# Decay sums and beta spread over the partitions through DRAM, Gram products turned, conv-state transposes merged

## What is computed

```python
q, k = l2_norm(q), l2_norm(k)                    # behind a causal conv of width 4 and SiLU
beta = sigmoid(b);  g = -exp(a_log) * softplus(a + dt_bias)
G = cumsum(g)                                    # within a chunk
decay = exp(where(causal, G[:, None] - G[None, :], -inf))
a_mat = where(strict, (beta * k) @ k.T * decay, 0)
u = solve(I + a_mat, v * beta)                   # lower triangular
w = solve(I + a_mat, k * beta * exp(G))
qk = (q @ k.T) * decay                           # q scaled by 128 ** -0.5
# then: v_new = u - w @ S;  o = (q * exp(G)) @ S + qk @ v_new;  S = S * exp(G_last) + kd.T @ v_new
```

## Time and profile before

| what | value |
|---|---|
| median of 3 runs | 1909.12 us (1908.06 to 1911.35) |
| the profiled execution | 1911.12 us, its span 1909.3 us |
| busy: PE, DVE, ACT | 1800.0, 556.5, 388.0 us |
| busy: weight loads, POOL | 933.9, 19.5 us |
| moved | 519.92 MB, mean 272 GB/s |
| chain that ended last | PE 79%, DMA 17%, DVE 2%, ACT 1% |

### The profile page before, as it was taken

One profiled execution on the slowest core, in us unless ns is written; L12 is line 12 of the kernel. 1 busy time (PEld: TensorE's weight loads), 2 busy tenths in 40 slices (PEclk: granted clock), 3 DMA queues, 4 the chain that ended last, 5 costly groups with the idle time before them and its releaser, 6 DMA issues.

```text
span 1909.3 us, 22816 instructions
## 1 busy us (share of the span) xinstructions
PE 1800.0 (94%) x8060; PEld 933.9 (49%) x8060; DVE 556.5 (29%) x1811; ACT 388.0 (20%) x922; POOL 19.5 (1%) x37
## 2 busy tenths in 40 slices
PE   7999999999998999999999999999999999999998
PEld 4777777777775433433333333333333333334333
DVE  2334434434434200321323213232132311224113
ACT  1424524524523111311000111001010010002103
POOL 0000000000000000000000000000000000000000
PEclk9999999999999999999999999999999999999999
DMA  8333433433404461599999999999999999999401
GB/s 253 100 95 102 126 94 103 124 94 104 124 28 149 152 250 73 199 419 428 427 428 427 427 427 427 427 427 427 428 426 427 425 427 425 424 424 384 168 22 50
DMA packets 208462, 519.92 MB, mean 272 GB/s; under 512 B 18664, under 2 KB 139488, under 8 KB 157152
## 3 DMA queue, kind: packets, MB, share of 16 engines
q1 hardware_dynamic: 198160, 513.83, 69.0%
q0 software_dynamic: 2304, 4.86, 0.7%
q10 hardware_dynamic: 7968, 0.83, 0.3%
HBM read 519.14 MB, written 12.26 MB: 278 GB/s over the span
## 4 chain that ended last, share of the span: by engine, by line
PE 79%; DMA 17%; DVE 2%; ACT 1%; issue 1%; SPq 0%; DVEq 0%; ACTq 0%
PE ps L582 75%; DMA ring<-in_w_down_dram 17%; PE ps L585 3%; DMA x<-in_x_sample_dram 0%; PE ps L1082 0%; ACT hb L1210 0%; ACT ring L1210 0%; SPq L477 0%; DMA pp_rows<-hb 0%; DVE ring L1694 0%; PE ps L710 0%; PE ps L730 0%; DVE ring L1745 0%; PE ps L731 0%; DVE x L2011 0%
## 5 line engine op out<-in xcount | busy, mean ns | idle before, releaser
L582 PE MATMUL ps<-ring,hT 128*64 128x512 f32 x2048 | 457.0, 596 | 25.6 <-DMA ring<-in_w_up_dram 25.6
L582 PE MATMUL ps<-hT,ring 128*128 128x288 f32 x1536 | 410.1, 414 | 0.0
L582 PE MATMUL ps<-ring,mixT 128*64 128x512 f32 (+2 forms) x1408 | 365.6, 598 | 35.9 <-DMA ring<-in_w_down_dram 25.6
L582 PEld LDWEIGHTS ps<-hT,ring 128*128 128x128 f32 x1536 | 283.3, 192 | 70.4 <-issue 0.5
L582 PEld LDWEIGHTS ps<-ring,hT 128*64 128x64 f32 x2048 | 145.7, 137 | 308.4 <-issue 305.8
L582 PEld LDWEIGHTS ps<-ring,mixT 128*64 128x64 f32 (+2 forms) x1408 | 124.8, 144 | 240.2 <-issue 238.3
L582 PE MATMUL ps<-ring,hb 128*128 128x512 f32 (+2 forms) x512 | 143.7, 512 | 0.0
L582 PE MATMUL ps<-mixT,wpT 128*128 128x512 f32 (+1 forms) x384 | 130.1, 601 | 0.0
L582 PEld LDWEIGHTS ps<-ring 128*128 128x128 f32 (+3 forms) x880 | 115.7, 186 | 29.0 <-DVE ring L1767 7.9
L582 PE MATMUL ps<-ring 128*128 128x128 f32 (+3 forms) x880 | 123.8, 272 | 1.7 <-DVE ring L1754 1.6
L1210 ACT ACTIVATE ring<-ps 128x256 f32<-128x256 f32 (+5 forms) x176 | 47.5, 310 | 294.4 <-PE ps L582 256.8
(11 more groups left out here) (248 smaller groups left out, 1096.7 us busy)
## 6 DMA issues: line engine op xcount, KB each, us to landing
ring<-in_w_gate_dram SPq DMA_DIRECT2D x128, 1024.0 KB, 22.5
ring<-in_w_up_dram SPq DMA_DIRECT2D x128, 1024.0 KB, 24.4
ring<-in_w_down_dram SPq DMA_DIRECT2D x128, 1024.0 KB, 22.0
ring<-in_w_in_dram SPq DMA_DIRECT2D x48, 1024.0 KB, 5.6
ring<-in_w_out_dram SPq DMA_DIRECT2D x16, 1024.0 KB, 11.0
ring<-in_w_ple_gate_dram SPq DMA_DIRECT2D x16, 1024.0 KB, 13.3
hb<-in_state_delta_dram SPq DMA_DIRECT2D x8, 512.0 KB, 5.2
out_dram<-hb SPq DMA_DIRECT2D x8, 512.0 KB, 3.7
```

The costliest lines, as they stand in the source:

```text
L582: return pe.matmul(out, lhsT, rhs, start=start, stop=stop)
```

## The change

The sums G and beta of all heads are turned in the preparation by six more matmuls (8 rows of 288 columns each), copied by DVE to gb_stage, stored by SP to a DRAM buffer gb_rows, and a head's two rows are loaded from there into all 128 partitions (Gb, 2304 bytes each): for the first head right behind the store, for the others in the head before, behind load_gate. With G along the row in SBUF, DVE makes dd and its mirror dT at the head's start, and ACT takes both exponentials.

The Gram products are now computed in turned form, one matmul per tile with k as weights and q and k side by side as 256 columns. DVE multiplies them with decay, beta along the row and masks, which gives the turned matrices (NTa, QKT) directly; X, which needs the other orientation only beside the diagonal, is built from the same product, since k k^T is symmetric, with the mask low0 folded into DL. The matmuls of gcol, the six transposes of Am and QKm, the wait for A_r, AT_mm, and ACT's copy of QKT go. PE's `next_head()` calls keep their counts, so 12 and 9 projection matmuls now stand together. The level masks of NT are made one level at a time (levels 0 to 2 before the loop of levels, then lev + 2 behind each lev_new), both tiles in one operation.

The conv-state rows of q, k and v lie one below the other on 72 partitions and are turned by one transpose; so do the new rows, 81 columns, turned by one; stores read them at partitions 27 s. The diff, cut to its core:

```diff
+        gb_rows = nc.dram_tensor("gb_rows", (HEADS, 2 * TOK), F32).ap()
+            def load_rows(h):
+                sp.dma_start(Gb.rearrange("p a n -> p (a n)"), gb_rows[bass.ds(h, 1), :].to_broadcast([P, 2 * TOK])
+                             ).then_inc(E["gb_ld"], 16)
...
                 sp.wait_ge(piece_mm, s + 1)
                 load_piece(s, P + piece_col[s])
+            sp.wait_ge(dec["prep_v"], 4)
+            sp.dma_start(gb_rows, gb_stage.rearrange("p a n -> p (a n)")).then_inc(E["gb_st"], 16)
+            sp.wait_ge(E["gb_st"], 16)
+            load_rows(0)
...
                     sp.wait_ge(E["mixA_r"], h1)
                     load_gate(h1)
+                    load_rows(h1)
                 piece(3)
...
-            mm(ps[0:SAMPLE, 3, 40:48], C("ball", SAMPLE), g[0:SAMPLE, 2, :]).then_inc(dec["prep_mm"], 1)
+            mm(ps[0:SAMPLE, 3, 40:48], C("ball", SAMPLE), g[0:SAMPLE, 2, :])
+            beta = pre[:, 3]
+            for t in range(2):
+                mm(ps[0:HEADS, 3, 64 + t * P:64 + (t + 1) * P], g[:, t, :], C("triu"))
+                mm(ps[0:HEADS, 2, t * P:(t + 1) * P], beta[:, t, :], C("ident"))
+            mm(ps[0:HEADS, 3, 64 + PROMPT:64 + TOK], g[0:SAMPLE, 2, :], C("btriu", SAMPLE))
+            mm(ps[0:HEADS, 2, PROMPT:TOK], beta[0:SAMPLE, 2, :], C("ident", SAMPLE, SAMPLE)).then_inc(dec["prep_mm"], 1)
...
-                for s in range(3):
-                    last = tr(ps[:, 2, s * 24:(s + 1) * 24], stt[0:SEQS * PAD, s, :], SEQS * PAD)
-                last.then_inc(E["st_T"], 1)
+                tr(ps[:, 2, 0:72], stt[0:72, :], 72).then_inc(E["st_T"], 1)
                 pe.wait_ge(E["cs_r"], h1)
-                for s in range(3):
-                    last = tr(ps[0:27, 4, s * P:(s + 1) * P], cs[:, s, :], P)
-                last.then_inc(E["cs_T"], 1)
+                tr(ps[0:81, 4, 0:P], cs[:, :, :].rearrange("p s c -> p (s c)"), P).then_inc(E["cs_T"], 1)
...
                 for t in range(2):
-                    kt, qt = qk[:, 1, t * P:(t + 1) * P], qk[:, 0, t * P:(t + 1) * P]
-                    mm(ps[:, 7, t * P:(t + 1) * P], kt, kt)
-                    mm(ps[:, 7, 256 + t * P:256 + (t + 1) * P], qt, kt)
-                    mm(ps[:, 2, t * P:(t + 1) * P], gcol[:, t, :], C("triu"))
-                kt, qt = qk[:, 1, PROMPT:TOK], qk[:, 0, PROMPT:TOK]
-                mm(ps[0:SAMPLE, 4, 0:SAMPLE], kt, kt)
-                mm(ps[0:SAMPLE, 4, SAMPLE:2 * SAMPLE], qt, kt)
-                mm(ps[:, 2, PROMPT:TOK], gcol[0:SAMPLE, 2, :], C("btriu", SAMPLE)).then_inc(E["tok_mm"], 1)
+                    mm(ps[:, 7, t * 256:(t + 1) * 256], qk[:, 1, t * P:(t + 1) * P], qk[:, :, t * P:(t + 1) * P])
+                mm(ps[0:SAMPLE, 4, 0:2 * SAMPLE], qk[:, 1, PROMPT:TOK], qk[:, :, PROMPT:TOK]).then_inc(E["tok_mm"], 1)
                 next_head()
-
-                pe.wait_ge(E["A_r"], h1)
-                pe.wait_ge(E["tok_cp"], h1)
-                pe.wait_ge(E["D_r"], h1)
-                for t in range(2):
-                    tr(ps[:, 5, t * P:(t + 1) * P], Am[:, t, :], P)
-                    tr(ps[:, 6, t * P:(t + 1) * P], QKm[:, t, :], P)
...
                 next_head()
...
                     if lev == 1:
                         pe.wait_ge(E["NT_r"], h1)
+                        pe.wait_ge(E["tok_cp"], h1)
...
-                f(eG, ps[:, 2, 0:TOK], ACT.Exp)
-                f(Dm[:, :, :], dd[:, :, :], ACT.Exp, scale=-1.0)
-                f(Ds[0:SAMPLE, :], dds[0:SAMPLE, :], ACT.Exp, scale=-1.0).then_inc(E["D_r"], 1)
+                f(eG, Gb[:, 0, :], ACT.Exp)
+                f(dd[:, :, :], dd[:, :, :], ACT.Exp, scale=-1.0)
+                f(dds[0:SAMPLE, :], dds[0:SAMPLE, :], ACT.Exp, scale=-1.0)
+                f(dT[:, :, :], dT[:, :, :], ACT.Exp)
+                f(dTs[0:SAMPLE, :], dTs[0:SAMPLE, :], ACT.Exp).then_inc(E["D_r"], 1)
+                act.wait_ge(E["tok_mm"], h1)
...
+            cp(gb_stage[:, 0, :], ps[0:HEADS, 3, 64:64 + TOK])
+            cp(gb_stage[:, 1, :], ps[0:HEADS, 2, 0:TOK])
...
-                for t, (_, n) in enumerate(TILES):
-                    ts(gcol[0:n, t, :], C("ones", n), hs[0:n, t, 0:1], None, ALU.mult)
+                v.wait_ge(E["gb_ld"], snap(h * 16 + 16))
+                for out, sample, clip in ((dd, dds, ALU.max), (dT, dTs, ALU.min)):
+                    for t in range(2):
+                        ts(out[:, t, :], Gb[:, 0, t * P:(t + 1) * P], hs[:, t, 1:2], 0.0, ALU.subtract, clip)
+                    last = ts(sample[0:SAMPLE, :], Gb[0:SAMPLE, 0, PROMPT:TOK], hs[0:SAMPLE, 2, 1:2], 0.0, ALU.subtract, clip)
+                last.then_inc(E["dd_r"], 1)
...
+                tt(CT[:, :, :], dT[:, :, :], both("triu"), ALU.mult)
+                tt(EB[:, :, :], dT[:, :, :], Gb[:, 1, 0:PROMPT].rearrange("p (t n) -> p t n", t=2), ALU.mult)
...
+                v.wait_ge(E["tok_mm"], h1)
+                gram = ps[:, 7, :].rearrange("p (t a n) -> p t a n", t=2, a=2)
+                tt(NTa[:, :, :], gram[:, :, 1, :], EB[:, :, :], ALU.mult)
...
+                    st(out=X[:, t, :], in0=gram[:, t, 1, :], scalar=hs[:, t, 2:3], in1=DL[:, t, :], op0=ALU.mult, op1=ALU.mult)
...
+                def masked(lev):
+                    return tt(NT[:, lev, :, :], NTa[:, :, :], both(f"mt{lev}"), ALU.mult)
...
+                tt(QKT[:, :, :], gram[:, :, 0, :], CT[:, :, :], ALU.mult)
+                tt(QKTs[0:SAMPLE, :], ps[0:SAMPLE, 4, 0:SAMPLE], CTs[0:SAMPLE, :], ALU.mult).then_inc(E["QKT_r"], 1)
+                masked(2)
...
+                    if lev + 2 < LEVELS:
+                        masked(lev + 2)
```

More of the change, by code:

```diff
@@ L191, in trunk @@
         qk = w(2, TOK)
-        gcol = w(3, P)
+        Gb = w(2, TOK)
         dd = w(2, P)
         dds = w(SAMPLE)
[L195 to L198, removed]
+        dT = w(2, P)
+        dTs = w(SAMPLE)
+        DL = w(2, P)
+        DLs = w(SAMPLE)
         eG = w(TOK)
         qg = w(TOK)
[L201 to L204, removed]
+        EB = w(2, P)
+        EBs = w(SAMPLE)
+        NTa = w(2, P)
+        NTas = w(SAMPLE)
         kbg = w(3, P)
@@ L230, in trunk @@
         cs = w(3, PAD + SEQS * PAD)
-        csT = w(3, P)
-        stt = w(3, P)
+        csT = w(P)
+        stt = w(P)
         vaT = w(TOK)
@@ L247, in trunk @@
         mA = ot
[L248 to L249 removed]
+        CT = w(2, P)
+        CTs = w(SAMPLE)
+        gb_rows = nc.dram_tensor("gb_rows", (HEADS, 2 * TOK), F32).ap()
+        gb_stage = Snew[0:HEADS, 0:5, :].rearrange("p a n -> p (a n)")[:, 0:2 * TOK].rearrange("p (a n) -> p a n", a=2)
         lnj = Vm[:, 0:3, :]
@@ L315, in trunk @@
                  "cs_cp", "cs_st", "va_st", "s2_st", "sn_st", "qkv_r", "sq_r", "ss_mm", "qk_r", "tok_mm", "dd_r", "D_r",
-                 "tok_cp", "A_r", "AT_mm", "QKT_r", "NT_r", "W_r", "dS_mm", "W_T", "WT_r", "Wrep", "WTs_r", "ln_d",
+                 "tok_cp", "gb_st", "gb_ld", "QKT_r", "NT_r", "W_r", "dS_mm", "W_T", "WT_r", "Wrep", "WTs_r", "ln_d",
                  "ln_sq", "vn_r", "mixA_mm", "mixA_r", "uw_mm", "uw_cp", "WQ_r", "S1_mm", "S1_r", "SQ_mm", "wS_mm",
@@ L1668, in _, with both @@
             n_before = ch.n
+            def both(name):
+                return C(name).unsqueeze(1).to_broadcast([P, 2, P])
             def head(h, loop):
@@ L1713, in head @@
                 tt(qk[:, 1, :], qkvT[:, 1, :], rn[:, 1, :], ALU.mult).then_inc(E["qk_r"], 1)
-                v.wait_ge(E["tok_mm"], h1)
-                for t in range(2):
-                    ts(dd[:, t, :], ps[:, 2, t * P:(t + 1) * P], hs[:, t, 1:2], 0.0, ALU.subtract, ALU.max)
-                ts(dds[0:SAMPLE, :], ps[0:SAMPLE, 2, PROMPT:TOK], hs[0:SAMPLE, 2, 1:2], 0.0, ALU.subtract,
-                   ALU.max).then_inc(E["dd_r"], 1)
                 v.wait_ge(E["qk_r"], h1)
@@ L1722, in head @@
                 tt(qg, qk[:, 0, :], eG, ALU.mult)
+                st(out=DL[:, :, :], in0=dd[:, :, :], scalar=-1.0, in1=both("low0"), op0=ALU.mult, op1=ALU.mult)
+                st(out=DLs[0:SAMPLE, :], in0=dds[0:SAMPLE, :], scalar=-1.0, in1=C("low0", SAMPLE, SAMPLE), op0=ALU.mult,
+                   op1=ALU.mult)
+                tt(CT[:, :, :], dT[:, :, :], both("triu"), ALU.mult)
+                tt(CTs[0:SAMPLE, :], dTs[0:SAMPLE, :], C("btriu", SAMPLE), ALU.mult)
+                tt(EB[:, :, :], dT[:, :, :], Gb[:, 1, 0:PROMPT].rearrange("p (t n) -> p t n", t=2), ALU.mult)
@@ L1723, in head @@
+                ch(tt(EBs[0:SAMPLE, :], dTs[0:SAMPLE, :], Gb[0:SAMPLE, 1, PROMPT:TOK], ALU.mult))
+                ch.wait()
+                v.wait_ge(E["tok_mm"], h1)
+                gram = ps[:, 7, :].rearrange("p (t a n) -> p t a n", t=2, a=2)
+                tt(NTa[:, :, :], gram[:, :, 1, :], EB[:, :, :], ALU.mult)
+                tt(NTas[0:SAMPLE, :], ps[0:SAMPLE, 4, SAMPLE:2 * SAMPLE], EBs[0:SAMPLE, :], ALU.mult)
                 for t in range(2):
-                    tt(DS[:, t, :], Dm[:, t, :], C("strict"), ALU.mult)
@@ L1728, in head @@
                 ch.wait()
```

(28 more changed lines are left out.)

18 lines of the change are left out of this document (6 added, 12 removed).

## The result

The changed kernel took 1903.99 us (median of 9 runs, 1902.08 to 1906.67) against 1909.12: ratio 0.9973, 95% interval 0.9963 to 0.9982, 5.1 us less. Forecast were 10.6 us less, with 1903.5 as the upper end. So the direction was right, the size about half. The first median lies 0.5 us beyond the range's upper end and the two others, 1901.41 and 1903.14, lie inside it, so the scatter of the medians alone could have put it on either side; what is missing from the forecast gain is told from the traces.

What follows compares the result with a forecast made beforehand. PE was taken to bound the heads, with expert loads released by its progress. Seven looped heads gain 10.5 us, the last 4.9, the first loses 4.8: 10.6 less, median 1898.5 us, range 1893.5 to 1903.5.

Steps and rivals of the forecast that it cites:

- Looped heads, tokens: Token part of each looped head: shorter Gram stretch gains 0.83 us, six transposes gone gain 0.69.
- Looped heads, start: Start of each looped head: two transposes fewer, -0.23 us; DVE's later cs_r, +0.25; net +0.02; sq_r wait stays shut.
- Row load in the loop: Loading the next head's rows inside the looped heads: one more SP issue and some 295 KB, cost 0.
- First head: Start of the first head: uncovered DRAM round trip of the rows delays PE, loss 4.8 us, bounds 3.0 and 8.
- Last head: Last head, qk_r to first level: waits A_r and NT_r, transposes and Gram time go; net gain 4.9 us.
- Rival (a): Clock falls at two or three head starts, 1.7 us each; last head 1.7 either way; 1902.5 us; chance 0.12.
- Rival (b): Clock falls at every head start, 2.1 us in each of seven heads; 1913.2 us; chance 0.05.
- (c): DVE bounds the heads: PSUM-priced operations or sq_r and NT_r waits open; 5 us less gain, 1903.5; chance 0.08.
- (d): First head's round trip long, 8 instead of 4.8 us, and late in the loop too; 1901.7 us; chance 0.07.
- (e): Gain doesn't reach the end, expert loads start by something else than PE; 0 to -2 us, 1908; chance 0.06.

Runs made afterwards that it cites:

- e7: Changed kernel with its Gram products as one matmul for each product (four of 128, two of 32 columns); 1902.69 us.
- e6: Changed kernel with the merging of the conv-state transposes undone: three each for old and new conv rows; 1903.02 us.
- e2: Changed kernel with two matmuls of 288 columns, result unread, put on PE ahead of the wait for cs_r; 1899.07 us.
- after: The changed kernel itself, against the kernel before the change; 1903.99 us.
- before: The kernel without the change, the reference of the comparison; 1909.12 us.
- e9: e8 with the projection matmul behind the output steps moved to ahead of the wait for va's piece at the head's start; 1876.95 us.
- e8: e3 with projection matmuls moved from behind tok_mm: one ahead of cs_r, one ahead of or_r, three ahead of sq_r in the last head; 1886.07 us.
- e5: Kernel before the change with three more unread DVE operations of 128 columns ahead of cs_r at each head start; 1911.89 us.
- e1: Changed kernel run once more, nothing altered; 1901.41 us.
- e10: Changed kernel run a third time, nothing altered; 1903.14 us.
- e3: Changed kernel with DVE's row-load wait and six dd and dT operations moved from the head's start to behind ln_d; 1892.59 us.
- e4: Kernel before the change with three unread matmuls of 288 columns added in each head behind the steps following tok_mm; 1918.78 us.

## Why the prediction was half right

The steps hold as follows.

- *Looped heads, tokens*: 0.83 + 0.69 forecast. The Gram stretch went from 2.01 to 1.19 us, the way from there to the first level from 11.09 to 10.29, and neither NT_r nor QKT_r was waited for. Right, and 0.1 us better than forecast. The cover was less than the 6.8 us of the forecast (10.2 less 3.4): DVE reached NT_r at 168.1, PE at 172.35, 4.2 us ahead. D_r did not come before tok_mm, as the prediction had it; ACT was held by table loads and a piece, and DVE's masks began at 163.29, 1.2 us behind the Gram stretch. That it is gcol's matmuls that pay, as the sum by columns had it, e7 shows.
- *Looped heads, start*: net +0.02 forecast. PE resumed 0.18 us after cs_r's transpose instead of 0.35, with a gap of 1.20 us instead of 0.71. DVE's six operations took 1.08 us (145.58 to 146.66), forecast 1.02. sq_r stayed shut. cs_r came 0.27 us later behind the head's first transpose, forecast 0.25; but of the 0.23 us of two transposes only 0.06 stayed, as e6 shows. The net was +0.21, and that a head still shrank by 1.46 us, where 1.50 were forecast, is in part luck: the tokens gave 0.1 more than forecast and the rest of the head 0.05.
- *Row load in the loop*: cost nothing. In the first head's turn it was issued at 126.37, 19 us ahead of its use at 145.58, and such a load landed in 4.1 us (median of eight).
- *First head*: forecast -4.8, measured -5.85 to cs_r. prep_v 4 came 3.99 us behind the preparation's mark, forecast 3.98. The store took 2.2 us from issue to the load's issue (68.08 to 70.27), forecast 1.4; the load 3.4, forecast 3.2. The term of the round trip was too small by 1 us. The further loss of the first head to the low clock, taken over as it was, came out 0.3 us smaller. The Trainium skill ("DMA: Bandwidth & Descriptors", Latency and other measured facts) with its fixed cost of about 2 us for a DMA was nearer for the store than the 1.4 us row of a 16 KB store inside a stream.
- *Last head*: forecast -4.9, measured -6.5, and -5.2 in e2 where the clock fell at the old place. The waits for A_r and NT_r went as said. The 1.6 us on top are no saving of the change: in after the clock fell behind sq_r, so the slow stretch lay under the wait for qk_r, which shrank from 2.05 us to 0.49. Rival (a) had this chance, 1.7 us either way. The clock there in the table by stretch, then PE's timeline of after:

```profile
581.00:582.00 1.00, 1.00 (x3) 0.69 (x3) 0.00 (x0) 0.98 (x5) 0.00 (x0) 0.50 1.04 406
```

```profile
580.59 2.22 PE L593 MATMUL ps<-ring,cst 128*128 128x288 f32 x4 [3.07 <-ACT ring L1209]
582.60 2.37 PE L593 MATMUL ps<-hT,ring 128*128 128x288 f32 x6
585.46 0.33 PE L743 MATMUL ps<-cst,ring 128*128 128x128 f32 x1 [0.49 <-DVE ring L1721]
...
592.80 0.78 PE L593 MATMUL ps<-ring 128*128 128x128 f32 x6
```

- *The step that failed* is the price of PE's longer wait for cs_r in "Looped heads, start": it was put down at its 0.25 us alone, with the clock at 1.00, and the fall of the clock was put among the rivals, as (a), with 0.12. The fall was what happened, in three heads, at the price given there: 3 x 1.68 = 5.0 us, which e2 gave back. With it the sum is 10.6 - 5.0 - 1.0 (first head) + 1.6 (last head) = 6.2 us, inside the three intervals. The evidence given against it, clock 1.00 in all looped heads of before, was evidence on gaps of 0.7 us only.
- A side error, in the section on the kernel before as well: the 0.6 us at L710 were put down to or_r. They are ACT's emptying of the last piece behind the last projection matmul, as e9 shows for the changed kernel. It changed nothing in the sum, but misplaced a matmul in e8.

Rival (b) would have needed a fall in all seven heads. (c) is out by the head length of 70.23 us. Of (d) only 1 us in the first head came true, and nothing in the loop. (e) is out by the table: behind the heads the trace of after loses nothing of its lead.

## What to carry to other kernels

A gap of PE that grows costs more than its length where it brings the clock down: here the falls stood behind gaps of 0.91 to 1.20 us and cost 1.7 us each. Such a gap needs that price as a rival with a real chance, or work put into it. Work that fills an engine's early part of a stage (dd and dT ahead of cs_r) belongs where that engine waits anyway; the same six operations 8 us later, where DVE waited for the norms, held up nothing, and the DRAM round trip was covered with them. Where PE has surplus cover at one wait and none at another, moving single matmuls between them gains their whole length, provided they stand behind the work that the wait's releaser itself needs.

## What the runs showed of the hardware

- PE's granted clock fell to 0.50 for 3.4 us behind gaps of only 0.91 to 1.20 us (with a wait of 0.58 us shortly ahead), in one to three of seven nearly equal places (e5, e6, after, e7), and in the same places in three traces of one program (after, e1, e10). Behind gaps of 0.71 us (before, e3, e4) it fell at none.
- Two dependent DMAs of 18 KB out and 288 KB in took 5.6 us from the first issue to DVE's first operation on the data (68.08 to 73.65).
- An fp32 matmul of 256 columns took about as long as two of 128 with the same weights (1.19 against 1.23 us for the whole Gram stretch of after and e7).
